# Both halves of the memory's V made during the first expert stage, and no memory rows kept in HBM

## The reference, cut to what matters

```
def cross_attention(hn, mem_n, w_cq, w_ckv, w_co):
    q = (hn @ w_cq).reshape(B, S, X_HEADS, X_HEAD_DIM)
    k, v = jnp.split((mem_n @ w_ckv).reshape(B, M, 2, X_HEADS, X_HEAD_DIM), 2, axis=2)
    ...
    s = jnp.einsum('bshd,bmhd->bhsm', q, k).astype(jnp.float32) * (X_HEAD_DIM ** -0.5)
    p = jax.nn.softmax(s, axis=-1).astype(v.dtype)
    o = jnp.einsum('bhsm,bmhd->bshd', p, v).reshape(B, S, X_WIDTH)
    return o @ w_co
```

## Time and profile before

| | before |
|---|---|
| median of three runs | 2263.84 us (2262.74 to 2271.11) |
| the profiled execution | 2264.59 us, of which the traced span is 2262.8 us |
| PE busy | 2131.7 us (94%) |
| DVE, ACT, POOL busy | 736.5, 389.2, 221.1 us |
| moved | 529.84 MB, mean 234 GB/s |
| PE's granted clock, mean | 0.984 |

### The profile page before, as it was taken

How to read it: one execution, slowest core, us unless ns; L and a number is a source line. 1 busy time by engine, 2 the same in 40 slices (tenths; PEclk the granted TensorE clock), 3 DMA queues, 4 the chain that set the end, 5 groups by cost and what they waited for, 6 DMA issues and landing times.

```text
span 2262.8 us, 27254 instructions
## 1 busy us (share of the span) xinstructions
PE 2131.7 (94%) x11665; PEld 1108.0 (49%) x11665; DVE 736.5 (33%) x1755; ACT 389.2 (17%) x736; POOL 221.1 (10%) x233
## 2 busy tenths in 40 slices
PE   8999799999988999889999899999999999998987
PEld 4454566654344333344556568854444533333332
DVE  4126676333101111031377853422222411111104
ACT  3101132121000100021133352210122200000101
POOL 5000312000000000000010133200000000000001
PEclk9999999999999999999999999999999999999999
DMA  8113113159999999994110201243343599999998
GB/s 310 38 38 112 38 38 138 71 236 387 423 428 427 424 427 427 425 376 139 29 30 2 77 2 38 75 157 113 112 183 133 208 411 426 427 428 427 427 425 337
DMA packets 96941, 529.84 MB, mean 234 GB/s; under 512 B 10286, under 2 KB 25827, under 8 KB 69418
## 3 DMA queue, kind: packets, MB, share of 16 engines
q1 hardware_dynamic: 82304, 492.08, 53.6%
q10 hardware_dynamic: 6346, 18.02, 2.2%
q0 software_dynamic: 8160, 17.88, 2.1%
HBM read 509.57 MB, written 30.93 MB: 239 GB/s over the span
## 4 chain that ended last, share of the span: by engine, by line
PE 77%; DMA 14%; DVE 5%; ACT 1%; SPq 1%; issue 1%; ACTq 0%; DVEq 0%
PE ps L204 73%; DMA RING<-in_w_e_up 4%; DMA RING<-in_w 3%; DMA SC<-in_w_e_up 2%; DMA XT<-in_w 1%; DMA SC<-in_w 1%; DMA EX<-in_w_e_up 1%; SPq L1626 1%; DMA RING<-in_w_ckv 1%; PE ps L1712 1%; ACT SC L1869 1%; PE ps L1760 1%; PE ps L375 0%; PE ps L2693 0%; PE ps L3288 0%
## 5 line engine op out<-in xcount | busy, mean ns | idle before, releaser
L204 PE MATMUL ps<-SC 64*64 64x64 f32 (+5 forms) x5360 | 747.8, 348 | 54.9 <-ACT SC L1869 11.7
L204 PE MATMUL ps<-RING,SC 128*64 128x512 f32 (+2 forms) x1664 | 581.2, 588 | 21.6 <-DMA SC<-in_w 5.6
L204 PEld LDWEIGHTS ps<-SC 64*64 64x64 f32 (+2 forms) x5360 | 324.8, 144 | 360.7 <-issue 302.5
L204 PE MATMUL ps<-XT,RING 128*128 128x512 f32 (+2 forms) x976 | 351.4, 514 | 3.1 <-DVE XT L200 1.1
L204 PEld LDWEIGHTS ps<-RING,SC 128*64 128x64 f32 (+2 forms) x1664 | 202.5, 152 | 255.7 <-issue 246.6
L204 PEld LDWEIGHTS ps<-XT,RING 128*128 128x128 f32 (+1 forms) x976 | 182.8, 191 | 144.8 <-issue 129.9
L1937 DVE SCALAR_TENSOR_TENSOR SC<-ps,ST,SC 128x512 f32<-128x512 f32 x30 | 22.5, 751 | 640.3 <-PE ps L204 640.3
L204 PE MATMUL ps<-RING,XT 128*128 128x512 f32 (+1 forms) x384 | 147.6, 545 | 0.0
L204 PE MATMUL ps<-SC,RING 128*128 128x512 f32 (+2 forms) x472 | 127.3, 436 | 2.3 <-DVE SC L1211 0.8
L204 PE MATMUL ps<-XT,SC 128*64 128x512 f32 (+2 forms) x280 | 111.5, 551 | 4.0 <-DMA SC<-in_w_e_up 3.3
L204 PEld LDWEIGHTS ps<-RING,XT 128*128 128x128 f32 x384 | 69.3, 195 | 76.5 <-issue 75.8
(11 more groups left out here) (470 smaller groups left out, 1922.8 us busy)
## 6 DMA issues: line engine op xcount, KB each, us to landing
SC<-in_w SPq DMA_DIRECT2D x49, 2048.0 KB, 30.6
RING<-in_w SPq DMA_DIRECT2D x35, 2048.0 KB, 32.7
RING<-in_w_in SPq DMA_DIRECT2D x16, 2048.0 KB, 8.9
SC<-in_w_e_gate SPq DMA_DIRECT2D x14, 2048.0 KB, 39.6
SC<-in_w_e_up SPq DMA_DIRECT2D x13, 2048.0 KB, 40.3
SC<-in_w_e_down SPq DMA_DIRECT2D x13, 2048.0 KB, 37.1
RING<-in_w_e_gate SPq DMA_DIRECT2D x11, 2048.0 KB, 40.4
RING<-in_w_e_up SPq DMA_DIRECT2D x11, 2048.0 KB, 41.1
```

Source lines behind the costliest of these rows:

```text
L204: return e.matmul(out, l, r, start=st, stop=sp, skip_group_check=True)
```

## The change

The first column half of V is no longer made in the attention but in expert stage 1, like the second. `mv_s`, `mv_p` and `mv_a` take a `half`: half 1 is loaded ahead of pair 3's weights (it was ahead of pair 4's) and made after pair 2 (it was after pair 3); half 0 is loaded ahead of pair 5's weights and made after pair 4. memV holds both halves. memT, its four writes and its read are gone, and so are the load of `cv0` in the second mixer, V's 16 matmuls in `cr_p` and the copy of V in each of `cr_a` and `cr_v`. The slot lists are adjusted for one load more in stage 1 and one less in the mixer.

```diff
-    memT = nc.dram_tensor("memT", [128, 4, 512], F, kind="Internal").ap()
-    memV = nc.dram_tensor("memV", [128, 2, 512], F, kind="Internal").ap()
+    memV = nc.dram_tensor("memV", [128, 2, 1024], F, kind="Internal").ap()
...
-        W.wait_ge(*ME.on("ev", "xt", 6))
-        W.wait_ge(*ME.on("ev", "xt", 7))
-        for n in range(4):
-            e.dma_start(memT[:, n, :], me_homes[n]).then_inc(*ME.up("dmt", "memT"))
...
+    def mv_p(e, c, half, n):
+
+        W.wait_ge(*slots.on(f"cv{half}"))
+        xt_ready(e, ME)
+        b, free = c.take("mv", half, n)
         W.wait_ge(*free)
         j, c0 = n // 2, n % 2 * 256
-        proj(e, b[:, 0:256], lambda k: me.dst[:, k, j * 128:(j + 1) * 128], lambda k: w8("cv1")[:, k, c0:c0 + 256], 8).then_inc(*c.up("p", "mv", n))
+        proj(e, b[:, 0:256], lambda k: me.dst[:, k, j * 128:(j + 1) * 128], lambda k: w8(f"cv{half}")[:, k, c0:c0 + 256], 8).then_inc(*c.up("p", "mv", half, n))
+
+    def mv_a(e, c, half, n):
+
+        j, c0, m = n // 2, n % 2 * 256, 4 * (1 - half) + n
         dst = CH[:, c0:c0 + 256]
-        if n >= 2:
-            W.wait_ge(*ME.on("memV", n - 2))
-        W.wait_ge(*c.on("mv", n))
-        copy_a(e, dst, c.at("mv", n)[:, 0:256]).then_inc(*c.up("a", "ev", "mv", n))
-        W.wait_ge(*c.on("ev", "mv", n))
-        e.dma_start(memV[:, j, c0:c0 + 256], dst).then_inc(*ME.up(f"dv{n % 2}", "memV", n))
+        if m >= 2:
+            W.wait_ge(*ME.on("memV", m - 2))
+        W.wait_ge(*c.on("mv", half, n))
+        copy_a(e, dst, c.at("mv", half, n)[:, 0:256]).then_inc(*c.up("a", "ev", "mv", half, n))
+        W.wait_ge(*c.on("ev", "mv", half, n))
+        e.dma_start(memV[:, j, 512 * half + c0:512 * half + c0 + 256], dst).then_inc(*ME.up(f"dv{n % 2}", "memV", m))
+
+    MV_LOADS, MV_AFTER = (6 * 3, 6 * 5), (2, 4)
...
-                if put_n == 6 * 4 and bi == 0:
-                    mv_s(e)
+                if bi == 0 and put_n in MV_LOADS:
+                    mv_s(e, 1 - MV_LOADS.index(put_n))
...
-                if bi == 0 and q == 3:
+                if bi == 0 and q in MV_AFTER:
                     for n in range(4):
-                        mv_p(e, c, n)
+                        mv_p(e, c, 1 - MV_AFTER.index(q), n)
...
-        slots.begin((0, 1, 0, 1, 0, 1, 2, 3, 0, 1, 2, 3, 0, 1, 2, 3))
+        slots.begin((0, 1, 0, 1, 0, 1, 2, 3, 1, 2, 3, 0))
...
-        wload(e, "cv0", t["w_ckv_2"][0], 1024, 512, (CR, ("w", "cv0")))
...
     def cr_p(e):
         c = CR
         yield
-        W.wait_ge(*CR.on("mem"))
-        for half in range(1):
-            W.wait_ge(*slots.on(f"cv{half}"))
-            for j in range(2):
-                b, free = c.take("v", half, j)
-                W.wait_ge(*free)
-                proj(e, b[:, :], lambda k: me_T[:, k, j * 128:(j + 1) * 128], lambda k: w8(f"cv{half}")[:, k, :], 8).then_inc(*c.up("p", "v", half, j))
-            c.also("p", "w", f"cv{half}")
         turn_p(e, cr)
         xt_ready(e, c)
...
-        for half in range(1):
-            W.wait_ge(*c.on("v", half, 0))
-            copy_a(e, cr_V[:, 0, half * 512:(half + 1) * 512], c.at("v", half, 0)[:, :]).then_inc(*c.up("a", "ev", "v", half, 0))
```

More of the change, by code:

```diff
@@ L1501, in mk_a @@
         dst = CH[:, n % 2 * 256:n % 2 * 256 + 256]
[L1502 removed]
+        W.wait_ge(*(ME.on("memV", n + 6) if n < 2 else ME.on("keysT", 0, n - 2)))
         W.wait_ge(*c.on("mk", n))
@@ L1506, in mk_a, with mv_s @@
         e.dma_start(keysT[:, 0, n * 256:(n + 1) * 256], dst).then_inc(*ME.up(f"dv{n % 2}", "keysT", 0, n))
-    def mv_s(e):
-        s, free = slots.put(slots.next(), "cv1", (M0, ("mv", 3)))
+    def mv_s(e, half):
+        s, free = slots.put(slots.next(), f"cv{half}", (M0, ("mv", half, 3)))
         for f in free:
             W.wait_ge(*f)
[L1513 to L1518, removed]
+        c0 = 1024 + 512 * half
+        e.dma_start(s.rearrange("p (k n) -> p k n", k=8), t["w_ckv_2"][0].rearrange("(k p) n -> p k n", p=128)[:, :, c0:c0 + 512]).then_inc(*slots.up(f"cv{half}"))
+    def mv_p(e, c, half, n):
+        W.wait_ge(*slots.on(f"cv{half}"))
+        xt_ready(e, ME)
+        b, free = c.take("mv", half, n)
         W.wait_ge(*free)
         j, c0 = n // 2, n % 2 * 256
-        proj(e, b[:, 0:256], lambda k: me.dst[:, k, j * 128:(j + 1) * 128], lambda k: w8("cv1")[:, k, c0:c0 + 256], 8).then_inc(*c.up("p", "mv", n))
-    def mv_a(e, c, n):
-        j, c0 = n // 2, n % 2 * 256
+        proj(e, b[:, 0:256], lambda k: me.dst[:, k, j * 128:(j + 1) * 128], lambda k: w8(f"cv{half}")[:, k, c0:c0 + 256], 8).then_inc(*c.up("p", "mv", half, n))
+    def mv_a(e, c, half, n):
+        j, c0, m = n // 2, n % 2 * 256, 4 * (1 - half) + n
         dst = CH[:, c0:c0 + 256]
-        if n >= 2:
-            W.wait_ge(*ME.on("memV", n - 2))
-        W.wait_ge(*c.on("mv", n))
-        copy_a(e, dst, c.at("mv", n)[:, 0:256]).then_inc(*c.up("a", "ev", "mv", n))
-        W.wait_ge(*c.on("ev", "mv", n))
-        e.dma_start(memV[:, j, c0:c0 + 256], dst).then_inc(*ME.up(f"dv{n % 2}", "memV", n))
+        if m >= 2:
[5 more added lines that the diff above has]
+    MV_LOADS, MV_AFTER = (6 * 3, 6 * 5), (2, 4)
     PICKS = ((8, 9, 11, 12, 14), (6, 7, 9, 10, 12, 13))
@@ L1901, in a @@
                 down_a(e, c, q, c.at)
-                if bi == 0 and q == 3:
+                if bi == 0 and q in MV_AFTER:
                     for n in range(4):
-                        mv_a(e, c, n)
+                        mv_a(e, c, 1 - MV_AFTER.index(q), n)
                 if bi == 0 and q == 6:
@@ L3532, in cr_p @@
             W.wait_ge(*c.on("ev", "q", 1, n))
-        W.wait_ge(*c.on("ev", "v", 0, 0))
-        W.wait_ge(*c.on("ev", "v", 0, 1))
+        W.wait_ge(*c.on("mem"))
         for u in range(NC_ + 3):
@@ L3563, in cr_a @@
         W.wait_ge(*TL.on("ya", 3))
-        W.wait_ge(*ME.on("memT"))
         for step in (("keysT", 0, 2), ("keysT", 0, 3), ("keysT", 1)):
             W.wait_ge(*ME.on(*step))
[L3567 to L3570, removed]
+        for m in (6, 7):
+            W.wait_ge(*ME.on("memV", m))
+        e.dma_start(cr_V, memV).then_inc(*c.up("dmem"))
         e.dma_start(SC[:, 2, :], keysT.rearrange("p a n -> p (a n)")).then_inc(*c.up("dmem", "mem"))
@@ L3605, in cr_v @@
         norm_v(e, cr)
-        for half in range(1):
-            W.wait_ge(*c.on("v", half, 1))
-            copy_v(e, cr_V[:, 1, half * 512:(half + 1) * 512], c.at("v", half, 1)[:, :]).then_inc(*c.up("v", "ev", "v", half, 1))
         turn_v(e, cr)
```

5 lines of the change are left out of this document (2 added, 3 removed).

## The result

The changed kernel takes 2271.49 us (median of 20 runs, 2264.8 to 2275.76), the kernel before 2263.57 us in 20 runs beside it (2260.2 to 2272.67). The ratio is 1.0026, 95% interval 1.0017 to 1.0034: 5.9 us slower, 3.9 to 7.7. It is small, and inside what I had called no change (0.5%), but it is a loss.

What follows compares the result with a forecast made beforehand. The prediction held that DMA's last load sets stage 1's end, PE is the chain up to stage 2, and stage 2 lasts as its loads. +6.4 - 5.8 + 2.8 = +3.4 us gave 2267.2 us by the median, range 2259 to 2272.

Steps and rivals of the forecast that it cites:

- the same within 0.5%: Whole kernel: time changes by no more than 0.5%, 11.3 us, which a measurement cannot tell from no change; chance 0.90.
- Stage 1, more to move: Expert stage 1: one more 2 MB load, 4.9 us, and four more writes, 1.5 us, delay its end: +6.4 us.
- The slots: Stage 1: loads already issued keep DMA busy while a V block frees no slot, 11 us to spare: 0.
- DMA runs dry: Rival, stage 1: DMA idles up to 11 us at each V block, up to 2289 us; late DMA or PE together 0.12.
- A gap in DMA: Stage 1 in the profile after: DMA stays at 1.00 throughout; a gap would show the prediction wrong.
- More for PE: Stage 1: the second V block, 14.0 us, is covered by PE's waits for weights: 0; uncovered, 7.6 us more.
- ACT: Stage 1: ACT's waits for V's writes do not make PE wait for the next pair's silu: 0.
- The attention: Attention: without V, PE waits for the norm and the transposes start at 1610.7 instead of 1616.5 us: -5.8 us.
- The clock: Attention: PE's clock falls to about half behind the new 7.7 us wait: +2.8 us, between 0 and 3.5.
- the hidden load: Rival, stage 1: DMA has slack and the load costs nothing; 2261 us, or 2258 without the clock; chance 0.08.
- V's whole time back: Rival, attention: the norm is ready earlier and all 13.7 us of V come back; 2256.5 us; chance 0.03.
- the attention does give something: Against the rival that the attention gives nothing and only +6.4 is left; 2270 us; chance 0.04.

Runs made afterwards that it cites:

- load_only: Changed kernel with half 0's weights loaded in stage 1 and thrown away, no second V block or its writes; ratio 1.0018 against the kernel before.
- attention_only: Kernel before with only the attention part changed: stage 1 makes half 1 only, the attention makes no V; 0.9992 (0.9980 to 1.0004), -1.8 us.

## Why the prediction was right, and where it was not

It said 2267.2 us, +3.4, within 2259 to 2272, the same within 0.5%. The kernel is at 2271.5 by its median and +5.9 by the ratio. "The same" was right. That the time lies in the range is in part luck: by the median it is 0.5 us inside the upper end, 0.5 us above the 2271 to which the forecast itself reached, and the term that it missed most was in no bound. The sum was 2.5 us too low against the ratio; the next is where.

*Stage 1, more to move: +6.4.* The stage is 7.0 us longer (5.8 to 8.8 in the seven kernels with both halves made and written in it). The load's 4.9 is confirmed by `load_only`, the writes have 0 to 1.5; 4.9 and the dip's 0.9 leave 1.2 us for the writes and all else.

*The slots: 0, measured 0.9 net* (0.6 to 2.4 in the kernels with both halves). This step failed. I argued at the V blocks, where DMA had 11 us in hand, and there nothing is lost (DMA at 1.01 from 640 to 720 us). The loss came near 800 us, far from either block, where SP stood 6.4 us longer at one slot. It is the "DMA runs dry" rival, to about a tenth of its 22 us at most and at a place that I did not look at. "DMA's share is 1.00 or 1.01 in every stretch" was said from three stretches, none of them between 760 and 920 us; the kernel before itself falls to 414 GB/s there. A gap in DMA was named as a sign of being wrong, and a dip to 0.95 is a weak form of it.

*More for PE: 0. Right:* the blocks lie in PE's waits, which shrank from 14.8 to 8.3 us. *ACT: 0. Right:* the silus behind the two blocks (pairs 3 and 5, at 619.98 and 680.68 us) waited 1.3 and 1.4 us for PE, so ACT was ready ahead of it.

*The boundary: not in the sum, measured +1.9,* and +1.7 more when the clock falls on the keys, 4 times in 6. This is the largest miss. The sum had the load for the keys as what ends the wait; it lands at 1012.7, as forecast (1013), but PE's branch past the overfull experts' code ends later, at 1014.37.

*The attention: -5.8. Right:* with the clock held up X to the first query is 6.1 us shorter. The wait was 6.4 instead of 7.7 us, and for DVE's L365 and not for ACT's L353: the first three transposes need only the tiles that are ready first.

*The clock: +2.8, measured 1.6 at the place and 1.7 in a stretch 99 us later.* The size was right, for half of it by luck.

In sum 7.0 + 1.9 + 1.1 (1.7 in 4 of 6) - 4.5 + 1.7 = 7.2 us by the places (-4.5 is 6.1 less the clock's 1.6), 5.9 (3.9 to 7.7) by the runs. Of the rivals, the hidden load is excluded (`load_only`), and so is V's whole time back; the attention does give something, though `attention_only`'s interval only just leaves zero open.

## What to carry to other kernels

Work that is moved into a stage for its idle PE time brings its weights along: where DMA sets that stage's end, here each 2 MB cost 4.9 us there, whatever PE had free. Work that is taken out may have been the cover of a chain of small steps; leave as much of it as the chain is long, here half, and move only the rest. And where one queue issues in order into a ring of slots, look for the cost of one entry more at every place where that queue waits, not just at the new one.

## What the runs showed of the hardware that I had not expected

- A wait of 2.3 to 2.6 us on PE that comes and goes with the length of its program and that the profile calls "issue" in five of six kernels. It ends 0.16 or 0.17 us behind a branch of PE's sequencer, which takes 6.1 to 6.3 us there instead of 3.6 to 4.5 and ends 2.5 to 2.6 us behind the start of a 16 KB instruction transfer. The same arithmetic in half as many instructions was without the wait.
- A stretch at half clock that followed another after 98.9 or 99.0 us in all seven kernels that had the first, and was absent in six of the seven that had not.
- The second mixer, with the same work for PE in all fourteen kernels, took 581.5 to 589.6 us: effects of 2 us have to be read at their place, not from a span.
